# Product-key query computed head by head in plain fp32, with selection and gathers regrouped around it

## What is computed

```python
q = (xb @ w_query).reshape(PEER_BLOCK, PEER_HEADS, 2, PEER_QDIM // 2)   # 8 heads, 2 x 128 columns
sc = jnp.einsum('thpd,hpkd->thpk', q, sub_keys)                        # 128 keys each half
sv, si = lax.top_k(sc, PEER_TOPK)                                      # 16 of 128, twice
cand = sv[:, :, 0, :, None] + sv[:, :, 1, None, :]                     # 256 sums
top_s, pos = lax.top_k(cand, PEER_TOPK)                                # 16 of them -> idx
g = softmax(top_s)
a = gelu(einsum('thkd,td->thk', expert_u[idx], xb))
out = einsum('thk,thkd->td', g * a, expert_v[idx])
```

## Time and profile before

| | us |
|---|---|
| time, median of 3 runs | 1986.43 |
| lowest and highest | 1984.07, 1989.04 |
| the profiled execution: span from first to last instruction | 1990.1 |
| TensorE busy (matmul) | 1587.0 (80%) |
| VectorE busy | 1122.1 (56%) |
| GpSimd busy | 923.5 (46%) |
| ScalarE busy | 436.1 (22%) |
| gathers from both tables | 541.36 MB of 648.25 MB |

### The profile page before, as it was taken

The page is one execution under the profiler, slowest core; times in us unless marked ns, Lnnn a source line. Parts: engine busy times, 40 slices in busy tenths (PEclk is TensorE's granted clock), DMA queues, the critical chain, the costliest instruction groups (busy, mean ns, idle before and its releaser), DMA issues.

```text
span 1990.1 us, 17044 instructions
## 1 busy us (share of the span) xinstructions
PE 1587.0 (80%) x5668; PEld 934.4 (47%) x5671; DVE 1122.1 (56%) x1533; ACT 436.1 (22%) x581; POOL 923.5 (46%) x1142
## 2 busy tenths in 40 slices
PE   6999999999567777777777777776776776689896
PEld 5998888889552223222222222322222222233475
DVE  4567646566784646646456465564655646442445
ACT  3445345334210111111101011010110101111253
POOL 0000000000577676586675866758667687573200
PEclk9999999999879999999999999999999999999998
DMA  6445535655689999999999999999999999998852
GB/s 204 158 152 169 169 127 181 220 170 169 254 316 422 396 423 402 421 405 398 423 399 408 417 405 422 398 399 420 402 422 403 402 422 386 423 421 330 315 169 85
DMA packets 130331, 648.25 MB, mean 326 GB/s; under 512 B 14124, under 2 KB 14232, under 8 KB 63720
## 3 DMA queue, kind: packets, MB, share of 16 engines
q0 software_dynamic: 74496, 541.36, 66.5%
q1 hardware_dynamic: 51408, 105.91, 15.9%
q10 hardware_dynamic: 4376, 0.29, 0.2%
HBM read 645.42 MB, written 2.10 MB: 325 GB/s over the span
## 4 chain that ended last, share of the span: by engine, by line
POOL 32%; PE 30%; issue 20%; DMA 9%; DVE 5%; ACT 1%; DVEq 1%; ACTq 1%; POOLq 0%
PE acc L1296 17%; POOL u_ring L404 11%; POOL v_ring L416 9%; POOL tick L415 7%; DMA v_ring<-in_peer_v_dram,idxv 6%; PE acc L1309 5%; POOL tick L403 5%; PE acc L1513 3%; DMA u_ring<-in_peer_u_dram,idxu 3%; DVE w_lo L754 1%; DVE u_ring L1120 1%; PE mix L1352 1%; ACT w_hi L455 1%; PE mix L1513 1%; PE mix L1362 0%
## 5 line engine op out<-in xcount | busy, mean ns | idle before, releaser
L1120 DVE CUSTOM_DVE_ANT_0 u_ring<-u_ring,xn 128x2048 f32<-128x2048 f32 x256 | 583.5, 2292 | 525.5 <-DMA u_ring<-in_peer_u_dram,idxu 525.2
L1513 PE MATMUL mix<-v_ring,diag 128*128 128x512 f32 x1024 | 487.3, 621 | 171.5 <-DMA v_ring<-in_peer_v_dram,idxv 169.6
L1513 PE MATMUL acc<-v_ring,diag 128*128 128x512 f32 x992 | 459.0, 609 | 156.0 <-DMA v_ring<-in_peer_v_dram,idxv 153.7
L1513 PEld LDWEIGHTS mix<-v_ring,diag 128*128 128x128 f32 x1024 | 191.1, 196 | 467.8 <-issue 249.3
L1513 PEld LDWEIGHTS acc<-v_ring,diag 128*128 128x128 f32 x992 | 182.4, 192 | 430.3 <-issue 257.1
L754 DVE TENSOR_TENSOR w_lo<-raw,w_hi 128x2048 fp32r<-128x2048 f32 x96 | 219.8, 2291 | 199.8 <-ACT w_hi L455 198.7
L404 POOL DMA_INDIRECT u_ring<-in_peer_u_dram,idxu x256 | 310.5, 1213 | 40.3 <-issue 32.4
L416 POOL DMA_INDIRECT v_ring<-in_peer_v_dram,idxv x256 | 273.0, 1067 | 39.0 <-issue 16.2
L636 ACT ACTIVATE diag<-ident,wgt 128x128 f32<-128x128 f32 x240 | 92.8, 399 | 880.0 <-PE mix L1513 470.1
L415 POOL TENSOR_TENSOR tick<-tick 128x1 f32<-128x1 f32 x256 | 176.2, 688 | 202.6 <-PE acc L1513 108.5
L455 ACT ACTIVATE w_hi<-raw 128x2048 fp32r<-128x2048 f32 x96 | 183.6, 1913 | 324.5 <-PE acc L1296 195.0
(11 more groups left out here) (255 smaller groups left out, 1048.3 us busy)
## 6 DMA issues: line engine op xcount, KB each, us to landing
raw<-in_w_in_dram SPq DMA_DIRECT2D x48, 1024.0 KB, 5.1
raw<-in_w_out_dram SPq DMA_DIRECT2D x16, 1024.0 KB, 5.2
raw<-in_peer_query_dram SPq DMA_DIRECT2D x16, 1024.0 KB, 5.3
raw<-in_w_ple_gate_dram SPq DMA_DIRECT2D x16, 1024.0 KB, 5.1
u_ring<-in_peer_u_dram,idxu POOLq DMA_INDIRECT x256, 15.2
v_ring<-in_peer_v_dram,idxv POOLq DMA_INDIRECT x256, 14.8
h<-in_x_dram SPq DMA_DIRECT2D x2, 1024.0 KB, 6.8
wple<-in_w_ple_dram POOLq DMA_DIRECT2D x1, 2048.0 KB, 18.0
```

The source lines that it names most:

```text
L1120: V.tensor_tensor_reduce(out=u_ring[:, k % DEEP, :], in0=u_ring[:, k % DEEP, :], in1=xn2[:, b, :], scale=1.0, scalar=0.0, op0=ALU.mult, op ...
L1513: ins = T.matmul(pairs[j // 2][:, (j % 2) * CW:(j % 2 + 1) * CW], diag[:, k % DEEP, :], v_ring[:, k % DEEP, j * CW:(j + 1) * CW], start=Fa ...
```

## The change

1. The query is no longer a split stage. The scaled tokens are kept in fp32 as `t_q`, and TensorE multiplies `raw` with them directly, head by head (256 columns), in plain fp32: 2 matmuls of 256 moving columns for each of the 16 slices of the contraction. `split_hi` and `split_lo` of 16 slices and four `t_hi` and `t_lo` parts go.
2. The first four heads (`EARLY`) are computed before the gathers' stage; heads 4 to 7 are computed between the rows of `down` in groups 0 to 3, one contraction step (two matmuls) after each row, and their scores in the group after.
3. VectorE selects group 0 as soon as the scores of head 0 are there, makes the 16 products of group 0, takes the scores of heads 1 to 3, makes the weights and then selects group 1.
4. GpSimd issues four v rows of group 0 ahead of the wait for group 1's indices, and in that step the v rows run four ahead of the u rows.
5. ScalarE copies each head's query (`take_query`), for heads 4 to 7 between `diags(g - 1)` and `gelu_of(g)` of groups 1 to 4.
6. Memory: `v_ring` moves onto `w_hi` and `w_lo`, `sc` and the gate's weights onto `t_hi` and `t_lo`. The third query chunk is loaded when head 3 has used its slices, the fourth when head 5 has, and the first two gate slices when head 7 has.

```diff
+                def query(hh, kts):
+                    c = hh // 2
+                    for kt in kts:
+                        q, k = kt // KQ, kt % KQ
...
+                        for a in range(2):
+                            n0 = (hh % 2) * 2 * P + a * P
+                            ins = T.matmul(q_bank(hh)[:, a * S:(a + 1) * S], raw[:, q, k, n0:n0 + P], t_q[:, kt, :],
+                                           start=(kt == 0 and a == 0), stop=(kt == KT - 1), skip_group_check=True)
+                        if kt == KT - 1:
+                            ins.then_inc(q_ready, 1)
+                        elif k == KQ - 1 and hh % 2 == 1:
+                            ins.then_inc(q_used, 1)
...
+                query(0, range(0, KQ))
+                transpose_h(ND - 1)
+                query(0, range(KQ, KT))
+                scores(0)
+                for hh in range(1, EARLY):
+                    query(hh, range(0, KQ))
+                    if hh > 1:
+                        scores(hh - 1)
+                    query(hh, range(KQ, KT))
+                scores(EARLY - 1)
...
+                        def between(k):
+                            if g < PH - EARLY:
+                                query(EARLY + g, (k,))
+                            if g > 0 and k == 1:
+                                scores(EARLY + g - 1)
...
+                def take_query(hh):
+                    act.wait_ge(q_ready, hh + 1)
+                    if hh >= 2:
+                        act.wait_ge(score_ready, hh - 1)
+                    act.activation(qt_of(hh), q_bank(hh).rearrange("p (a t) -> p a t", t=S), ACT.Copy).then_inc(qt_ready, 1)
...
+                take_query(0)
                 softmax_top(0)
+                for hh in range(1, EARLY):
+                    take_query(hh)
                 gelu_of(0)
-                with act.Fori(1, G - 1) as g:
+                for g in range(1, 1 + PH - EARLY):
+                    softmax_top(g)
+                    diags(g - 1)
+                    take_query(EARLY + g - 1)
+                    gelu_of(g)
+                with act.Fori(1 + PH - EARLY, G - 1) as g:
                     softmax_top(g)
                     diags(g - 1)
                     gelu_of(g)
...
+                normed(0)
+                take_scores(0)
+                dve.drain()
+                top_k(0)
+                dve.drain()
+                current_top(0)
+                normed(1)
+                products(0, 0)
+                for hh in range(1, EARLY):
+                    take_scores(hh)
                 weights(0)
+                dve.drain()
+                top_k(1)
...
+                def one_group(g, b, more=None):
+                    dve.drain()
+                    current_top(g)
+                    top_k(g + 1)
+                    products(g, b)
+                    if more is not None:
+                        take_scores(more)
+                    weights(g)
+
+                one_group(1, 0)
+                for hh in range(EARLY, PH):
+                    one_group(hh - EARLY + 2, 0, hh)
...
+                    if ahead:
+                        pool.wait_ge(idx_moved, g)
+                        tock(3)
+                        for k in range(ahead):
+                            fetch_v(g, e, k)
                     if up:
                         pool.wait_ge(idx_ready, g + 1)
...
-                        if down and i >= lead:
...
+                        if down and lead <= i < TOPK + lead - ahead:
+                            fetch_v(g, e, i - lead + ahead, last)
...
-                pool.wait_ge(slice_used, NQ * gG)
-                step(1, 1, True, True)
+                step(1, 1, True, True, ahead=DEEP)
```

More of the change, by code:

```diff
@@ L378, in tock, with fetch_v, step @@
                     nc.gpsimd.tensor_tensor(tick[:, c:c + 1], tick[:, c + 4:c + 5], tick[:, c + 4:c + 5], ALU.add)
-                def step(g, e, up, down, lead=0, last=False):
+                def fetch_v(g, e, k, last=False):
+                    if not last or k < DEEP:
+                        pool.wait_ge(v_free, (g - 1) * TOPK + k + 1)
+                    elif k in dve_picks:
+                        pool.wait_ge(v_free_dve, k // DEEP)
+                    else:
+                        pool.wait_ge(v_free, free_before(k))
+                    nc.gpsimd.tensor_tensor(tick[:, 2 * k + 1:2 * k + 2], tick[:, 2 * TOPK + 4:2 * TOPK + 5], tick[:, 2 * TOPK + 5:2 * TOPK + 6], ALU.add)
+                    nc.gpsimd.indirect_dma_start(
+                        v_ring[:, k % DEEP, :], None, v_rows,
+                        bass.IndirectOffsetOnAxis(idxv[:, e, k:k + 1], 0)).then_inc(v_in[k % DEEP], 16)
+                def step(g, e, up, down, lead=0, last=False, ahead=0):
                     if down:
@@ L392, in step @@
                         tock(2)
-                    if down:
+                    if down and not ahead:
                         pool.wait_ge(idx_moved, g)
@@ new lines, in scores @@
+                def scores(hh):
+                    pe.wait_ge(keyst_ready, 1)
+                    pe.wait_ge(qt_ready, hh + 1)
+                    if hh == 0:
+                        pe.wait_ge(acc_free[1], gG // 2)
+                    if hh >= 2:
+                        pe.wait_ge(score_taken, hh - 1)
+                    for b in range(NB):
+                        for a in range(2):
+                            ins = T.matmul(score_bank(hh)[:, (b * 2 + a) * P:(b * 2 + a + 1) * P], qt_of(hh)[:, a, b * P:(b + 1) * P],
+                                           keyst[:, hh * 2 + a, :], start=True, stop=True)
+                    ins.then_inc(score_ready, 1)
@@ L1515, in down, with query_between @@
                             ins.then_inc(v_free, 1)
-                    with pe.Fori(b * PH, (b + 1) * PH - 2 * (b == NB - 1)) as g:
+                            if between is not None:
+                                between(k)
+                    def query_between(g):
+                        def between(k):
[3 more added lines that the diff above has]
+                                scores(EARLY + g - 1)
+                        return between
+                    if b == 0:
+                        for g in range(PH - EARLY + 1):
+                            down(g, range(TOPK), between=query_between(g))
+                    with pe.Fori(b * PH + (PH - EARLY + 1) * (b == 0), (b + 1) * PH - 2 * (b == NB - 1)) as g:
                         down(g, range(TOPK))
```

211 lines of the change are left out of this document (87 added, 124 removed).

## The result

The changed kernel takes 1993.4 us (median of 15 runs, 1988.0 to 1999.3) against 1987.6 us for the kernel before (15 runs): ratio 1.003, 95% interval 1.0018 to 1.0042. That is slower by some 6 us: the interval leaves out 1, and the size is just within the 6 us that the prediction called no difference. The forecast was 1987. One timed run of the whole study, an execution of e2 that took 8863 us, is left out of its ratio; nothing on record explains it.

A forecast was written before the change was run, and what follows sets the result against it. From about 580 us the gathers, filling the DMA engines, were taken to bound the kernel. On the profiled execution 1990.1 - 35 + 20 + 14 + 2 = 1991.1, median 3.7 lower: 1987 us; 8-in-10 range 1963 to 2004.

The forecast's parts named there:

- Start of the gathers: From the output projection's end to group 1's weights: indices come earlier, weights at 629 against 663.65; gain 35 us (27 to 42).
- a ring turn of 13: Group 0's u rows: four rows taken as 13 us without splits and scores, where 15.9 us was seen before.
- ScalarE's order: Boundaries of groups 2 to 4: query copy, waiting for TensorE, delays table load and gelu; 6.7 us each, 20 us lost.
- The drain behind the table load: ScalarE at boundaries: the skill's about 1380 ns would make each 8.1 us, total 4 us more; prediction kept 6.7.
- Loads in the saturated stretch: Fourth query chunk and two gate slices move to where gathers fill the DMA engines; five at 2.9, 14 us lost (10 to 16).
- colder TensorE: TensorE rows after waits at three boundaries run slower; mostly hidden by the ring, 2 us lost (0 to 8).
- Ten later groups and the end: Gate, final stages and memory moves: the same waits as before, 0 us (-2 to 2).
- Rival 1: Boundaries don't grow: last product comes after TensorE's last query step, or table load precedes the copy; 1967 us, chance 27%.
- Rival 2: `down` of groups 0 to 3: TensorE becomes the bound through cold rows, about 4 us more per boundary; 2003 us, 23%.
- Rival 4: Interleaving does nothing useful, query stage was hidden anyway; first u issue stays near 500; 2017 us, chance 5%.

The follow-up runs named there:

- e2: Changed kernel with all four slices of the first gate chunk, not only the last two, waiting for the last v row; 2001.5 us, ratio 1.0064.
- e1: Changed kernel with ScalarE doing the gelu before it copies the head's query in groups 1 to 4; 1976.3 us, ratio 0.9934.
- e9: Changed kernel with gelu before copy, group 1 selected inside group 0's dots, six heads ahead, scores of heads 2 to 4 taken between products; 1959.1 us, ratio 0.9857.
- e10: e9 with seven heads ahead of the gathers' stage instead of six; 1978.2 us, ratio 0.9956.
- e8: Changed kernel with all eight heads ahead of the gathers' stage and group 1 selected inside group 0's dots; 1995.1 us, ratio 1.0033.
- e5: e1 with six heads ahead of the gathers' stage instead of four; 1994.5 us, ratio 1.0026.

## Why the prediction was right

The forecast of 1987 for a median of 1986.4 was "no difference", within 6 us; measured were +5.8, so the size is right by a hair, and the sign of what little there is was not forecast. Against the span of 1990.1 my sum gave 1991.1; measured 1994.7, and without the 3.8 us of the dense stage, which are not the change's, it would be 1998.5. The sum of the terms was +1 and is +8.5: the start gave 2.1 less than forecast, the stalls cost 1.2 less, the loads and the slower TensorE together 3.3 more, and the stages behind, put at 0, cost 3.4. That the result fell inside the 6 us is in part luck: all terms but the stalls erred to the slow side, 7.5 us in sum in this pair of profiles. The two large ones, the start and the stalls, came out nearly as forecast. By its steps:

- **Start of the gathers, -35.** Measured -32.9 (222.3 to 189.4). The prediction's own terms for group 1 (553.5 + 67 + 7 + 2.3) add up to 630 and not 629, so one of the 2.1 us is arithmetic. The parts fit closely when the 3.8 us of the dense stage are allowed for: indices 469.2 forecast, 465.3 + 3.8 = 469.1 measured; end of the 16 products 531, 529.0 + 3.8 = 532.8; end of TensorE's first row 553.5, 550.5 + 3.8 = 554.3; weights of group 1 629, 626.9 + 3.8 = 630.7. Most of the products came every 3.24 us, a ring turn of 13, as chosen between 10 and 15.9.
- **ScalarE's order, +20.** Shown by the rows and by e1. From the end of the last product to the gelu are 7.0, 6.8 and 6.8 us at the three boundaries, where 6.7 stood for each; taking the copy away gave 8.1, 6.0 and 4.7, 18.8 us by the periods and 19 by the ratios. GpSimd's tick after u3 waited 14.97 us at the boundary of group 2, where 15 was forecast. Group 1 had no stall, as forecast: its copy ran at 619.11 and its gelu at 626.64. The drain behind the table load that the prediction quoted from the Trainium skill ("ScalarE: Activation LUTs", section "What ACT_TABLE_LOAD costs") isn't in the trace: 725.04 + 1.28, and the gelu starts at 726.34.
- **Loads in the saturated stretch, +14, and colder TensorE, +2.** Together they are what e1's four periods keep above those of before, 19.3 us instead of 16. How it divides is open. At e2's price of 2.35 us a slice, where 2.9 was taken, the five slices are 11.8 us and 7.5 are left for TensorE. But e2 was measured beside boundaries that stalled; e9 holds the two gate slices and a head's query between g1 and g2, e10 neither, and they differ by 5.6 us, which is up to 2.8 a slice, 14 for five, and leaves 5.3. Single rows of 5.4 to 6.7 instead of 3.67 us stand after the waits of the changed kernel, at a granted clock of 0.50 over 632 to 636, so a colder clock is there. Whether anything waited for it is another matter: in e1's period from g1 to g2 (second row), which is 9.8 us longer than before (first row), the DMA engines are as full as before. That speaks for the loads:

```profile
663.40:745.21 81.81, 60.40 (x128) 23.65 (x128) 46.17 (x75) 9.28 (x21) 57.24 (x71) 0.98 0.99 407
```
```profile
631.50:723.12 91.62, 73.34 (x188) 36.01 (x188) 46.08 (x75) 9.66 (x22) 61.97 (x78) 0.91 0.99 398
```

- **What is left without either.** e8 and e10, with no query and no slice between g1 and g5, are 2.7 and 2.2 us above the four periods of before in sum. Moving the gate's slices out saves the period and loses the end (e2).
- **Ten later groups and the end, 0.** Measured +1.5 and +1.9; no cause was looked for.

Rival 1 (boundaries don't grow) is refuted by the rows at 719 to 726 and by e1. Rival 2 (TensorE the bound) can hold no more than the 5 to 8 us that the loads leave above, where 16 were its price: most rows take 3.6 + 0.86 us and TensorE waits again after them. Rival 4 fell with the first issue at 468.4.

## What to carry to other kernels

When the gathers fill the DMA engines, a head start and a boundary are paid in the same coin: 33 us won at the start were lost again in the next four periods, about half of it in ScalarE's stalls and most of the rest in loads that had moved there. Before work is slipped into an engine's gaps, look at what stands behind its hand-over on the next engine: here a 0.6 us copy in front of a gelu cost 19 us, and a full pair of score banks with two more heads behind it made the start 29 us longer (e5 against e1). On an engine that runs in program order, the operation that others wait for comes first, and the one that itself waits long comes after it.

## What the runs showed of the hardware

- GpSimd's `tick` takes 0.19 us when VectorE is idle and up to 2.3 us while VectorE makes a product. "GPSIMD Engine Reference" of the Trainium skill, section "Specifications", has the two engines share their SBUF interfaces, with contention for VectorE instructions with two SBUF inputs; the two inputs of a product fit that. The first row is before a product is running, the others beside one, in the changed kernel:

```profile
468.10 0.19 POOL L455 TENSOR_TENSOR tick<-tick 128x1 f32<-128x1 f32 x1
...
523.65 2.11 POOL L422 TENSOR_TENSOR tick<-tick 128x1 f32<-128x1 f32 x1
526.89 2.12 POOL L422 TENSOR_TENSOR tick<-tick 128x1 f32<-128x1 f32 x1
```

- A 1 MB slice from SyncE's queue lands 11.1 us after its issue in the changed kernel (median of the 16 query slices), against 5.3 before, when most were issued beside half-idle DMA engines; what it takes from the gathers is less, 2.35 us by e2 and at most 2.8 by e9 against e10.
- TensorE's granted clock was 0.94 in one execution and 1.00 in the other over the same 60 us of the same stage, at full busy time both, and 277 and 292 of its matmuls lie in them. The table loads of ScalarE that stand 28.8 us apart at the higher clock stand 32.1 apart at the lower; no edit explains these 3.3 us, which are as much as some of the terms above.
